# S5 scans: two of the four products that turn a quad's inputs move from VectorE to GpSimd

## The reference, cut to what matters

```python
def s5_scan(u, lam_bar, b_bar, c_mat, h0):
    bu = jnp.einsum('gpj,blgj->blgp', b_bar, u.astype(jnp.complex64))
    bu = bu.at[:, 0].add(lam_bar[None] * h0)
    a = jnp.broadcast_to(lam_bar, bu.shape)
    _, hs = lax.associative_scan(_lin_rec, (a, bu), axis=1)
    y = jnp.einsum('gjp,blgp->blgj', c_mat, hs).real
    return y, hs[:, -1]
```

## Time and profile before

| | us |
|---|---|
| median of 3 runs | 4552.39 (4549.79 to 4558.13) |
| the profiled execution | 4547.74 |
| its span, first to last instruction | 4546.0 |
| S5 scans within the span | 444.4 to 674.6 |

### The profile page before, as it was taken

One profiled execution on the slowest core, in us unless ns is written; L12 is line 12 of the kernel. 1 busy time (PEld: TensorE's weight loads), 2 busy tenths in 40 slices (PEclk: granted clock), 3 DMA queues, 4 the chain that ended last, 5 costly groups with the idle time before them and its releaser, 6 DMA issues. The chain is left out here.

```text
span 4546.0 us, 44442 instructions
## 1 busy us (share of the span) xinstructions
PE 4260.6 (94%) x15674; PEld 2495.8 (55%) x15674; DVE 2948.2 (65%) x5912; ACT 749.5 (16%) x1571; POOL 1619.1 (36%) x1471
## 2 busy tenths in 40 slices
PE   7898559999999999999998998899999999999998
PEld 3563344768554555545546886476855455554553
DVE  5444972899976766647644316599997676664763
ACT  2120451018100000000002223101810000000000
POOL 0000510019566655536500000001956665553640
PEclk9999779999999999999999999899999999999999
DMA  4120542127899999979931112212789999997993
GB/s 174 51 77 23 189 183 99 52 88 206 317 366 365 405 367 356 364 290 397 369 126 56 69 37 45 81 56 84 209 327 360 365 408 372 356 361 288 405 361 121
DMA packets 354409, 1048.58 MB, mean 231 GB/s; under 512 B 31657, under 2 KB 132361, under 8 KB 342234
## 3 DMA queue, kind: packets, MB, share of 16 engines
q0 software_dynamic: 148096, 545.34, 31.5%
q1 hardware_dynamic: 107036, 450.27, 26.4%
q10 hardware_dynamic: 99072, 50.33, 3.9%
HBM read 991.69 MB, written 54.14 MB: 230 GB/s over the span
## 5 line engine op out<-in xcount | busy, mean ns | idle before, releaser
L592 PE MATMUL banks<-blocks,picked_T 128*128 128x512 f32 x3072 | 1361.0, 595 | 16.0 <-DVE picked_T L772 16.0
L555 PE MATMUL banks<-h_dense_T,blocks 128*128 128x384 f32 x4096 | 1357.6, 486 | 0.0
L555 PEld LDWEIGHTS banks<-h_dense_T,blocks 128*128 128x128 f32 x4096 | 776.9, 190 | 581.9 <-issue 98.6
L592 PEld LDWEIGHTS banks<-blocks,picked_T 128*128 128x128 f32 x3072 | 586.6, 191 | 712.8 <-issue 658.7
L383 POOL DMA_INDIRECT expert_rows<-in_pk_u_dram,expert x512 | 670.6, 1310 | 478.3 <-DVE own_dots L787 253.2
L383 POOL DMA_INDIRECT expert_rows<-in_pk_v_dram,expert x512 | 607.5, 1187 | 507.1 <-DVE acc L806 255.3
L806 DVE SCALAR_TENSOR_TENSOR acc<-expert_rows,expert_weight,acc 128x1024 f32<-128x1024 f32 x504 | 623.2, 1282 | 73.8 <-DMA expert_rows<-in_pk_v_dram,expert 73.1
L787 DVE CUSTOM_DVE_ANT_0 expert_rows<-expert_rows,h_rows 128x1024 f32<-128x1024 f32 x512 | 601.4, 1221 | 59.1 <-DMA expert_rows<-in_pk_u_dram,expert 57.8
L772 DVE TENSOR_TENSOR picked_T<-dense_act,shared 128x384 f32<-128x384 f32 x246 | 210.0, 854 | 563.6 <-PE banks L592 555.2
L408 ACT ACTIVATE dense_act<-banks 128x384 f32<-128x384 f32 x246 | 120.8, 491 | 2231.7 <-PE banks L555 2221.7
L374 POOL TENSOR_SCALAR expert_rows<-iota,picked_T 128x128 f32<-128x128 f32 x384 | 250.4, 670 | 474.0 <-ACT picked_T L414 415.9
(11 more groups left out here) (468 smaller groups left out, 3944.2 us busy)
## 6 DMA issues: line engine op xcount, KB each, us to landing
blocks<-in_pk_u_turned_dram SPq DMA_DIRECT2D x256, 512.0 KB, 6.6
blocks<-in_pk_v_dram SPq DMA_DIRECT2D x256, 512.0 KB, 6.7
gates_dram<-shared ACTq DMA_DIRECT2D x48, 1024.0 KB, 5.3
shared<-gates_dram SPq DMA_DIRECT2D x32, 1536.0 KB, 11.1
ada_block<-in_ada_rest_dram SPq DMA_DIRECT2D x32, 1280.0 KB, 7.6
blocks<-in_pk_w_q_dram SPq DMA_DIRECT2D x32, 512.0 KB, 3.3
MIXT<-in_ev_w_in_dram SPq DMA_DIRECT2D x16, 512.0 KB
expert_rows<-in_pk_u_dram,expert POOLq DMA_INDIRECT x512, 8.4
```

What stands on the lines that cost most here:

```text
L555: mm = pe.matmul(dense_dots(c), u[:, k * P:(k + 1) * P], HT[:, k, :], start=(k == 0), stop=(k == KD - 1))
L592: mm = pe.matmul(ps[:, at_:at_ + HALF], wt[:, c % WEIGHED, z * P:(z + 1) * P], v[:, half_ * HALF:(half_ + 1) * HALF], start=(c == 0), stop ...
```

## The change

GpSimd gets a function `turn_in(m)`, called behind `decays(m)`. It waits for all eight locals of quad m (`l_set`), for both tables of the quad, and for the end of quad m-1 (`prev_set`; in quad 0 for readouts(0), `c_set`), since the tiles W[2] and W[3] serve other steps before. Then it makes W[2] and W[3], four instructions, each of which counts `by_pool`. VectorE's turn_in makes only W[0] and W[1], and waits for `by_pool` before the sums.

```diff
+            def turn_in(m):
+
+                b = m % 2
+                pool.wait_ge(l_set, 8 * m + 8)
+                pool.wait_ge(table_set, 2 * m + 2)
+                if m:
+                    pool.wait_ge(prev_set, m)
+                else:
+                    pool.wait_ge(c_set, 1)
+                for w, part, f in ((W[2], 1, trig[:, b, 0]), (W[3], 0, trig[:, b, 1])):
+                    for a, z in PARTS:
+                        pool.tensor_tensor(w[:, :, a:z], L[:, part, :, a:z], f[:, :, 0:z - a],
+                                           ALU.mult).then_inc(by_pool, 1)
+
             for m in range(QUADS):
                 angles(m)
                 line.settle()
                 decays(m)
+                turn_in(m)
...
                 times(W[0], L[:, 0], cos)
                 times(W[1], L[:, 1], sin)
-                times(W[2], L[:, 1], cos)
-                times(W[3], L[:, 0], sin)
+                dve.wait_ge(by_pool, 4 * m + 4)
                 line.settle()
```

More of the change, by code:

```diff
@@ L1580, in s5 @@
 def s5(nc, T, ps, US, before, MIXT, room, ident, s, out_re, out_im, cond_s, mod, glu_w, glu_b, glu_in):
-    with stage(nc, "steps_in", "dve_line", "act_line", "pool_line", "cleared", "b_set", "diag_set", "c_set", "a_set", "angle_set", "table_set", "t_raw",
+    with stage(nc, "steps_in", "dve_line", "act_line", "pool_line", "by_pool", "cleared", "b_set", "diag_set", "c_set", "a_set", "angle_set", "table_set", "t_raw",
                "t_set", "e_raw", "l_set", "k_raw", "m_set", "l_used", "scan_done", "prev_set",
@@ L1587, in s5 @@
                "ada_in1", "ada_used", "ada_copied", "mod_out0", "mod_out1", "ones_set") as (
-            ctx, (steps_in, dve_line, act_line, pool_line, cleared, b_set,
+            ctx, (steps_in, dve_line, act_line, pool_line, by_pool, cleared, b_set,
                   diag_set, c_set, a_set, angle_set, table_set, t_raw, t_set, e_raw, l_set, k_raw,
```

## The result

The change makes the kernel slower, as forecast: 4573.68 us (median of 5 runs, 4572.85 to 4575.60) against 4553.2 for the kernel before on the same chip; ratio 1.005, 95% interval 1.0038 to 1.0061. The forecast was 4576, with 4560 to 4586. The span of the profiled execution is 4571.1 us instead of 4546.0.

The account below looks back on a forecast made before the run. VectorE was taken as the bound, with a TensorE and ScalarE chain close behind. Later quad starts plus 2.5 us in quad 3 gave +23.5 us on 4547.74, so 4571, plus 4.7 for the median: 4576 us, range 4560 to 4586.

Parts of the forecast that it names:

- The products: In turn_in, GpSimd's 5.5 us and VectorE's 3.0 us take turns: 8.5 us instead of 5.97, 2.5 us more per quad.
- The angles in front of c_set: Angles(m+1) now run behind turn_in(m), against adds and readouts: 8.5 + 10.4 + 11.6 = 30.5 us to TensorE's inside, before 16.4.
- The chain behind c_set: From TensorE's first inside product to ScalarE's last copy of the locals: 27.6 us in quad 1, 27.9 in quad 2.
- Quad 0: turn_in(0) starts at 484.4 instead of 493.5, but angles(1) last until about 514, so turn_in(1) starts at 530.8 against 531.40.
- The scan beside GpSimd: In quad 0, scans were taken as held up by GpSimd's angles; if not, all that follows comes 5.5 us earlier.
- VectorE's wait before the products: VectorE idle 5 to 6 us before the products of quads 1 to 3, waiting for ScalarE's copies of the locals.
- The back half of every scans at 10 to 11 us: Sign expected in the changed profile: VectorE's time from the end of the scans to the end of the quad, 10 to 11 us.
- The sum: turn_in(1), (2), (3) at 530.8, 588.9, 647.3, plus 2.5 us in quad 3: the stage ends 23.5 us later.
- Rival A: Engines run side by side, so GpSimd's products don't hold up VectorE's: 17 us faster, 4536 us; chance 5%.
- B: Rival: VectorE stays the bound because the chain behind c_set is shorter: +4.4 us, 4557 us; chance 8%.
- C: Rival: worse than the sum, more than one GpSimd instruction per handover or a dearer product, beyond 4586 us; chance 7%.

Follow-up runs that it names:

- e3: The changed kernel, but VectorE waits for GpSimd's products before making its own two; 4569.19 us, ratio 1.0039 to the kernel before.
- e5: e4 with the change put in: GpSimd makes the products W[2] and W[3] and has no angles; 4545.41 us, ratio 0.9987 to the kernel before.
- e6: e4 with steps loaded earlier, quad 0's angles on GpSimd in the convolution stage, and looser waits of inputs(0) and readouts(0); 4528.29 us, ratio 0.9950 to the kernel before.
- e4: The kernel before, products unchanged on VectorE, with all angles moved from GpSimd to VectorE; 4541.39 us, ratio 0.9974 to the kernel before.

## Why the prediction was right, step by step

- **The products, 8.5 us instead of 5.97.** Measured: GpSimd's four take 8.41 to 8.45 in all four quads, and quad 3 is 2.5 us longer (34.6 us from turn_in to the last states, 32.1 before). The mechanism holds: 6.05 alone (e3) and 3.03 alone (e5) make 9.1, of which 0.6 overlap at the handovers. That the sum fits is luck in part: GpSimd's share was put 0.5 too low (alone, its wide products take 2.36 us and its narrow ones 0.73, where 2.2 and 0.55 were said), and the overlap, which the prediction left out, made up for it. The rule itself, that instructions of the two engines which read SBUF take turns, is too wide: L1454 in e6 reads one input from SBUF and is not held up. Here it cost nothing, since the products, sums, scans and readouts of the S5 stage have both inputs in SBUF.
- **The angles in front of c_set, 30.5 us from turn_in to inside.** 30.2 in quads 1 and 2; the sums and readouts took 21.5 (said: 22).
- **The chain behind c_set, 27.6 and 27.9 us.** 27.2 and 27.4. A quad of 57.5 where 58 was said.
- **Quad 0.** With the late start taken off, turn_in(0), predicted at 484.4, came at 484.4, angles(1) lasted until 514.9 (said: about 514), ScalarE's wait for them was 9.4 us (8.7), with none before the tables of quads 2 and 3, and turn_in(1) came at 532.1 (530.8). The help of the early start was given back, as said.
- **The scan beside GpSimd,** on which the trace of before was silent, is held up. The scans of the changed kernel, one by one (duration in ns, least, median and most):

```profile
L2029 DVE TENSOR_TENSOR_SCAN s_w<-s_decay,s_w x8: 2797/2824/4471, 500.3 to 669.8; 128x1280 f32<-128x1280 f32 x8
```

  The two of quad 0 take 8.84 us, all others 2.8 each. VectorE and GpSimd in that moment:

```profile
500.33 8.84 DVE L2029 TENSOR_TENSOR_SCAN s_w<-s_decay,s_w 128x1280 f32<-128x1280 f32 x2
```

```profile
500.23 1.90 POOL L1702 TENSOR_TENSOR norm_rows<-s_steps,s_turns 128x1024 f32<-128x1024 f32 x1
502.20 4.29 POOL L1703 TENSOR_TENSOR norm_rows<-s_steps,s_turns 128x1024 f32<-128x1024 f32 x1
506.57 4.74 POOL L1704 TENSOR_TENSOR norm_rows<-norm_rows 128x1024 f32<-128x1024 f32 x1
```

  The first scan is recorded from 500.33, but ends only at 504.8, 2.7 us after the end of L1702 at 502.13; L1703 waits for that and ends at 506.49; the second scan ends 2.7 us behind that, at 509.17, and L1704 after it. The Trainium skill (SBUF — State Buffer, "Who interferes with whom") says that a VectorE instruction with two SBUF inputs contends with a GpSimd instruction that reads SBUF; the scan is such a one, and the trace agrees, 4.47 us against 2.80.
- **VectorE's wait before the products, said to be 5 to 6 us.** 7.9 before quad 1, 4.9 and 4.7 before quads 2 and 3. In quad 0 VectorE is through about when it was said, and the locals come 1.3 us later.
- **"The back half of every scans at 10 to 11 us"** was wrong for quad 0: 15.8 us (509.21 to 525.05), since the last of angles(1), which the prediction itself let run until 514, and the decays stand beside it. It holds for quads 1 to 3 (11.0, 11.0, 10.0). It cost nothing, for VectorE waited 7.9 us behind it.
- **The sum, +23.5 us.** The stage has 23.6. The span of the profiled execution rose by 25.1 and the median by 20.5, with an interval of the ratio that reaches from 17 to 28 us; the forecast of 4576 lies 2.3 us above the median. The agreement within 0.1 us is luck in part: turn_in(1) came 1.3 us later than said, and quads 1 and 2 were 0.7 and 0.8 us shorter.

Rival A (side by side) was to be told by a wide product of VectorE beside GpSimd's, 1.2 us or 3.4. It took 1.75, and the narrow one behind GpSimd's first wide product up to 2.57, where 0.42 is its length alone: the waiting falls on both kinds. A falls with the four together, 6.27 us where 3.03 is their length alone, and with e5. B (VectorE the bound) needed a chain behind c_set of much less than 27 us; it took 27.2 and 27.4, and VectorE waited ahead of every quad. C had no sign: the two engines' products alternate one to one, and the time lies below 4586.

## What to carry to other kernels

Before work is moved from VectorE to GpSimd, price it as if both ran on one engine wherever GpSimd reads SBUF and VectorE's instructions have both inputs there (or are a tensor_scalar, as in e5, 2.74 us where 0.69 alone): in a stage bound by VectorE the move costs about the difference of the two durations (here 2.5 us, where the products take 6.05 us alone on GpSimd and 3.03 on VectorE), and work already on GpSimd can be worth taking back (e4) or moving to a stage where VectorE reads PSUM and has time to spare (e6). Look then at GpSimd's queue: what stands behind the new instructions is delayed by their waits, and here that was the larger part of the loss, 14 of 24 us. A chain with a little to spare, here 6.7 us behind c_set, becomes the bound as soon as more than that is put in front of it, here 13.8 us.

## What the runs showed of the hardware

VectorE's products with one input in PSUM were not held up by GpSimd (e6: 0.68 us), one with both inputs in SBUF was (2.83 for 0.68). The eight angles took 15.2 to 22.0 us on GpSimd by what VectorE ran beside them: 15.2 beside products most of which read PSUM (e6), 17.5 beside sums and readouts (changed kernel, quads 1 and 2), 18.1 beside products and sums (e3), 22.0 beside sums and two scans (changed kernel, quad 0). In e4, VectorE's two-input L1911 took 1.23 us beside GpSimd's memset, as it does alone, but the one-input tensor_scalar behind it (L1912) 2.15 us where it takes 0.69 alone (in e5 1.23 and 2.11). So an instruction of GpSimd that only writes held up the tensor_scalar and not the product. The Trainium skill (SBUF — State Buffer, "Who interferes with whom") has both: a tensor_scalar may go in a mode that takes the shared ports for reading and writing, a two-input instruction contends only with GpSimd's reads; this trace agrees with 2.15 against 0.69 and with 1.23, which are times and do not show the mode.
